# A hybrid decoder layer: eight gate tiles ahead of attention by four units of seven products, and attention's steps rearranged

## What is computed

```python
proj = u @ w_in                      # xp | q | k | v | gate_logits (2 x 1024)
y_pool = causal_pool_mixer(xp, ...) @ w_branch_pool
# strictly causal stick-breaking attention, per head and row block:
z = q @ k.T * scale
log_a = log_sigmoid(z) + cumsum_from_right(log_sigmoid(-z)) - log_sigmoid(-z)
o = where(mask, exp(log_a), 0) @ v
y_sb = o @ w_branch_attn
g_pool, g_sb = split(sigmoid(gate_logits))
h = h + (g_pool * y_pool + g_sb * y_sb) @ w_out
```

## Time and profile before

| | us |
|---|---|
| median of 3 runs (1916.88 to 1917.36) | 1917.23 |
| the profiled execution | 1917.42 |
| its span, first to last instruction | 1915.6 |
| TensorE busy | 1904.6 (99%) |
| VectorE busy | 1371.4 (72%) |
| ScalarE busy | 795.7 (42%) |
| POOL busy | 117.6 (6%) |
| attention, from the first to the last gate matmul | 240.0 |

### The profile page before, as it was taken

The page is one execution under the profiler, slowest core; times in us unless marked ns, Lnnn a source line. Parts: engine busy times, 40 slices in busy tenths (PEclk is TensorE's granted clock), DMA queues, the critical chain, the costliest instruction groups (busy, mean ns, idle before and its releaser), DMA issues.

```text
span 1915.6 us, 24977 instructions
## 1 busy us (share of the span) xinstructions
PE 1904.6 (99%) x9010; PEld 1593.2 (83%) x9010; DVE 1371.4 (72%) x1677; ACT 795.7 (42%) x1175; POOL 117.6 (6%) x157
## 2 busy tenths in 40 slices
PE   9999999999999999999999999999999999999998
PEld 9888888888888888888888888898888888888887
DVE  6978777784565786488677768889777777756555
ACT  7423232323434544234676762474323232324344
POOL 1000000000000200000233220010000000000002
PEclk9999999999999999999999999999999999999999
DMA  5456654558676733415875447643545444677665
GB/s 165 144 199 229 224 181 140 199 188 303 213 237 203 196 110 132 132 50 160 247 173 148 128 142 257 198 138 119 178 145 194 149 168 153 218 263 244 205 193 205
DMA packets 258419, 348.24 MB, mean 182 GB/s; under 512 B 29344, under 2 KB 161184, under 8 KB 255008
## 3 DMA queue, kind: packets, MB, share of 16 engines
q1 hardware_dynamic: 258336, 347.15, 56.2%
HBM read 233.83 MB, written 112.99 MB: 181 GB/s over the span
## 4 chain that ended last, share of the span: by engine, by line
PE 96%; DVE 1%; SPq 1%; DMA 1%; issue 0%; ACT 0%; POOL 0%; POOLq 0%; DVEq 0%; ACTq 0%
PE bank L1265 40%; PE bank L1321 8%; PE bank L1322 8%; PE bank L1323 8%; PE bank L1374 8%; PE bank L1515 6%; PE bank L1217 3%; PE bank L1451 2%; PE bank L1423 2%; PE bank L1481 2%; PE bank L1587 2%; PE bank L1192 1%; PE bank L1606 1%; PE bank L1605 1%; PE bank L1572 1%; PE bank L1570 1%
## 5 line engine op out<-in xcount | busy, mean ns | idle before, releaser
L2255 DVE TENSOR_TENSOR dn_lo<-dn_lo_raw,dn_hi 128x1024 fp32r<-128x1024 f32 x149 | 181.7, 1222 | 149.9 <-ACT dn_hi L1790 149.5
L1265 PE MATMUL bank<-lo_t,wa_hi 128*128 128x512 f32 x656 | 252.8, 389 | 0.0
L1265 PE MATMUL bank<-hi_t,wa_hi 128*128 128x512 f32 x656 | 252.8, 389 | 0.0
L1265 PE MATMUL bank<-hi_t,wa_lo 128*128 128x512 f32 x656 | 252.8, 389 | 0.0
L1790 ACT ACTIVATE dn_hi<-dn_lo_raw 128x1024 fp32r<-128x1024 f32 x149 | 157.9, 1061 | 219.0 <-DMA dn_lo_raw<-act_dram 219.0
L1321 PE MATMUL bank<-dn_hi 128*128 128x512 f32 x596 | 232.6, 390 | 0.0
L1323 PE MATMUL bank<-dn_lo,dn_hi 128*128 128x512 f32 x596 | 231.9, 389 | 0.0
L1322 PE MATMUL bank<-dn_hi,dn_lo 128*128 128x512 f32 x596 | 231.9, 389 | 0.0
L1265 PE MATMUL bank<-hi_b,wa_hi 128*128 128x512 f32 x492 | 190.6, 389 | 0.9 <-DVE up L2389 0.9
L1265 PE MATMUL bank<-hi_b,wa_lo 128*128 128x512 f32 x492 | 190.4, 389 | 0.0
L1265 PE MATMUL bank<-lo_b,wa_hi 128*128 128x512 f32 x492 | 190.4, 389 | 0.0
(11 more groups left out here) (275 smaller groups left out, 3750.9 us busy)
## 6 DMA issues: line engine op xcount, KB each, us to landing
wa_lo_raw<-in_ffn_w_gate_up_dram SPq DMA_DIRECT2D x87, 512.0 KB, 5.0
dn_lo_raw<-act_dram SPq DMA_DIRECT2D x149, 256.0 KB, 4.4
act_dram<-g SPq DMA_DIRECT2D x44, 512.0 KB, 4.5
wd_t<-in_ffn_w_down_dram SPq DMA_DIRECT2D x44, 512.0 KB, 6.6
act_dram<-s_of SPq DMA_DIRECT2D x88, 256.0 KB, 6.5
wd_dram<-wd_t SPq DMA_DIRECT2D x22, 1024.0 KB, 6.0
dn_lo_raw<-wd_dram SPq DMA_DIRECT2D x85, 256.0 KB, 3.3
dn_lo_raw<-in_ffn_w_down_dram SPq DMA_DIRECT2D x64, 256.0 KB, 3.0
```

The source lines that it names most:

```text
L1265: last = nc.tensor.matmul(acc, lhs, rhs, start=n == 0 and i != 2 and i < 5, stop=n == 11, skip_group_check=True)
L2255: return nc.vector.tensor_tensor(dst, raw, hi.bitcast(f32), ALU.subtract)
```

## The change

`EARLY` goes from 4 to 8: all eight tiles of the attention gate come out of mix units (four gate units instead of two), and the sixteen banks that stay in attention are all gates of the pool branch. A fourth row buffer `a3` is added and `LAG` is 3: transposes, `at_hi` and `at_lo` of a tile come three steps behind its logits instead of two, and the weighing moves with them. VectorE does `at_lo` ahead of the scan in every step. The shares of the first three steps, of the steps with value work on VectorE and of the last steps are raised. The first keys of the first head are loaded by ScalarE's queue instead of SP's, and the last pool branch tiles are stored ahead of a gate weight's load. In the first feed-forward VectorE's first Strassen pair is written out in an order of its own.

```diff
-EARLY = 4
+EARLY = 8
...
-DRAIN = 4
-V_DIFF, V_HIGH, V_LOW = ({NT + 3 + d: 1, 3 * NT + 3 + d: 2, 5 * NT + 3 + d: 3} for d in (0, 1, 5))
+DRAIN = 5
+LAG = 3
+V_DIFF, V_HIGH, V_LOW = ({NT + 4 + d: 1, 3 * NT + 4 + d: 2, 5 * NT + 4 + d: 3} for d in (0, 1, 2))
...
-HEAD_SHARE = 16
+HEAD_SHARE = 28
...
-    shares = [SHARE[x["qt"]] for x in TILES] + [7] * DRAIN
+    shares = [SHARE[x["qt"]] for x in TILES] + [12] * DRAIN
     shares[0] += HEAD_SHARE
-    shares[1] += 8
+    shares[1] += 14
+    shares[2] += 8
+    for s in (*V_DIFF, *V_LOW):
+        shares[s] += 5
...
+        a3 = at("a3", [P, SEQ], f32, G0)
...
-                    for dst, part in ((k_hi2, 0), (k_lo2, 1)):
+                    for dst, part in ((k_hi2, 0), (k_lo2, 1)) if hn or c0 else ():
...
+            spill_pool_branch(3)
             gate_unit(1)
-            spill_pool_branch(3)
             load_head(1)
...
             def weights_of(n):
-                return a2[:, :] if n % 3 == 2 else a[:, n % 3, :]
+                return (a[:, 0, :], a[:, 1, :], a2[:, :], a3[:, :])[n % 4]
...
-                if s >= 4 and s % 2 == 0:
-                    weigh((s - 4) // 2)
-                if 2 <= s < NA + 2:
-                    turn(s - 2)
+                if s >= LAG + 2 and s % 2:
+                    weigh((s - LAG - 2) // 2)
+                if LAG <= s < NA + LAG:
+                    turn(s - LAG)
...
+            def load_first_keys():
+
+                for i in range(3):
+                    act.wait_ge(ring_sp[i], 32 * ring_uses(i))
+                act.wait_ge(pool_prod, 6 * (KT // 2 - 1) + 3)
+                for dst, part in ((k_hi2, 0), (k_lo2, 1)):
+                    for half in (slice(0, 64), slice(64, P)):
+                        act.dma_start(dst[half, 0, 0:HALF].bitcast(f32),
+                                      qk_dram[part, PAIR_ORDER[0], 0:64, SEQ:SEQ + HALF]).then_inc(head_in[0], 16)
+
+            load_first_keys()
...
-                if n >= 3:
-                    act.wait_ge(t_ok, CHUNKS[n - 2])
+                if n >= 4:
+                    act.wait_ge(t_ok, CHUNKS[n - 3])
...
-                    with dve.Fori(1, WO_PAIRS + 1) as i:
+                    first_strassen_pair(even, odd, units)
+                    with dve.Fori(2, WO_PAIRS + 1) as i:
...
+            def first_strassen_pair(even, odd, units):
+
+                c11(0, 2, 0)
+                weight_sums(0, 3, odd, units + 2)
+                c22_first(0, 2, 0)
+                weights_lo(0, 3, odd)
+                c22_second(0, 2, 0)
+                sums_lo(0, 3, odd)
+                unit_end(0, 2, 1, 0, 0)
+                up_unit(0, 3, 1, 1, more=(even, units + 3), use=1)
...
-                turned_first = 2 <= s <= NA and TILES[s - 1]["qt"] in (1, 5, 3)
-                if turned_first:
-                    turned_lo(s - 2)
+                if LAG <= s < NA + LAG:
+                    turned_lo(s - LAG)
                 if 1 <= s <= NA:
                     weigh_keys(s - 1)
-                if 2 <= s < NA + 2 and not turned_first:
-                    turned_lo(s - 2)
```

More of the change, by code:

```diff
@@ L1108, in _ @@
                         store_gate(fb)
-                    if s == NA:
+                    if s == NA + 1:
                         move_o(NA // 2 - 2, 3, slice(0, HALF // 2))
-                    elif s == NA + 2:
+                    elif s == NA + 3:
                         move_o(NA // 2 - 1, 4, slice(HALF // 2, HALF))
-                    elif s >= 4 and s % 2 == 0:
-                        store_o((s - 4) // 2)
+                    elif s >= LAG + 2 and s % 2:
+                        store_o((s - LAG - 2) // 2)
                     if s == O_STEP:
@@ L1118, in _ @@
                             sp_.wait_ge(o_sp[b], 32 * (NA // 4 - 2))
[L1119 to L1122, removed]
+                    if O_STEP <= s < O_STEP + 5:
+                        load_output(s - O_STEP, slice(0, P if s < O_STEP + 3 else 64))
                     if s == NA:
@@ L2204, in _ @@
             for s in range(NA + DRAIN):
[L2205 to L2208, removed]
+                if s >= LAG + 2 and s % 2:
+                    take_o((s - LAG - 2) // 2)
+                if LAG <= s < NA + LAG:
+                    turned_hi(s - LAG)
                 if s < NA:
```

## The result

The changed kernel takes **1923.36 us** (median; 1921.34 to 1924.02) against 1917.07 (1916.74 to 1917.36) of the kernel before, measured beside it: ratio 1.0031, 95% interval 1.0022 to 1.0040, **6.3 us slower**. The forecast was 2.1 us faster, and the time lies outside its range.

What follows compares the result with a forecast made beforehand. TensorE's list of matmuls was taken as the time. Products -5.44, first pair -1.11, present waits -1.54 and new waits +6.0 gave -2.1 on 1917.42: 1915.3, median 1915.1 us; forecast's own range 1913.4 to 1919.6, 8 in 10 1910.3 to 1919.6.

Steps and rivals of the forecast that it cites:

- Products, mix units, first pair: Gate products leave attention, two gapless mix units added: net -5.4 us; reordered first Strassen pair in first feed-forward: -1.1 us.
- third rival: Added mix units wait for stores of reused ring tiles, losing 1 to 2 us each: 1918; chance 0.04.
- Start of attention, 0.5 us: ScalarE's first weight copy waits for its late transfer, with the transposes' copies queued behind it: 0.5 us.
- The clock: TensorE's granted clock should stay at its upper level, 2.4 GHz, since no wait is longer than a step.
- key wait: At attention's start, the 0.6 us wait on a key transfer goes once ScalarE issues the first four.
- Steady waits, 1.6 + 1.6 + 1.8 + 0.5: Waits through attention: weighing of fifth and sixth tile, two wide tiles in a row, value splits, VectorE scans running long.
- Place A: Weighing of a head's fifth and sixth row tile: short by 0.2 us a head, 1.6 in all.
- Place B: Two wide tiles in a row, a head's first and second: short by 0.2 us, 1.6 in all.
- the splits: Three value splits on VectorE in attention: 0.8 us short each, partly caught by slack, 1.8 us in all.
- The first, VectorE keeping up: Rival: mean load of 89% leaves room, attention's waits stay at 4.2 us or less, 1910.7; chance 0.36.
- The second: Rival: POOL's 16 products collide with VectorE's scans in attention, 16 us of waits, 1925; chance 0.08.
- the tenths recur eight times: Argument against VectorE keeping up: places A and B fall short by tenths, repeated over the eight heads.

Runs made afterwards that it cites:

- a_start: Changed kernel with the start of attention as before (keys back on SP ahead of queries, gate weights ahead of last pool stores): 1924.71 us.
- a_early4: Changed kernel with four gate tiles ahead of attention instead of eight, the rest as changed: 1913.16 us against 1917.18 of the kernel before, ratio 0.9980.
- a_late2: Changed kernel with ScalarE's four copies of gate unit 1's weights one step later: 1920.60 us.
- a_dose: The changed kernel with weight copies one step later, plus every fourth gate matmul of attention run twice (96 matmuls more): 1931.78 us.
- a_late: Changed kernel with ScalarE's four copies of gate unit 1's weights moved later, first piece at gate matmul 44 instead of 26: 1925.91 us.
- a_idle: Changed kernel with VectorE's scans cut to 128 columns per row tile and ScalarE's first sigmoid to 128 per chunk: 1916.88 us.

## Why the prediction was wrong

- **Products, mix units, first pair.** Right: 24 matmuls fewer, 152.3 us of mix stage, 1.0 to 1.1 us for the pair. The third rival (waits in mix units) didn't occur.
- **Start of attention, 0.5 us.** This term failed first. I had the right queue (a late transfer, the weight copy, the `at_hi` behind it) and gave it at most twice the 0.56 us of the earlier trace rows. The copy waited 3.42, TensorE 2.53 plus 1.7 for the clock, plus 1.5 on `q_st`: 5.7 us in the profile. The term has no length for the transfer, which took 7.2 us before; with four stores ahead of it and ScalarE's keys beside it, it took 10.7. And I had not set the thin opening against SP's timetable: whatever SP sends last arrives too late for it, as a_start shows.
- **The clock.** It was to stay at its upper level, "since no wait is longer than a step". A wait of 2.53 us, not longer than a mean step (23.4 / 8 = 2.9 us), was followed by 3.4 us at half of it, a loss that the forecast had at nothing.
- **`q_st`.** The key wait of 0.6 went, but what is late next is the query transfer, at 1.5. Moving the keys to another queue won nothing: TensorE starts its second logits 4.66 us after the start of attention here, and also 4.66 in a_start, with the keys on SP. The DMA share is 1.02 to 1.14 in that stretch (946 to 960).
- **Steady waits, 1.6 + 1.6 + 1.8 + 0.5.** 5.5 us were forecast and some 12 came. Place A, the weighing of the fifth and sixth tile, was the wrong place: it waits in two heads only (0.4 and 0.6). In a head where it does not wait (transposes at 1021.70), the `at_lo` ends 1.75 us behind the transposes (1023.94 against 1022.19), just as before and in spite of the scan ahead, with 1.94 of cover. The transposes just ahead of that weighing come 0.23 late in every head, 1.8 us, and the weighing of the last two tiles costs 0.46 in six heads and 1.1 in the first, 3.9 us; I had neither. Place B cost some 1.1 us in the seven heads behind the start's hole and the splits some 2, near what I had; the weighing of a head's first two tiles, 0.8 in all, I had not. And I counted a wait as the lateness of one matmul: a late weighing also costs 0.1 on the next, and transposes inside a set lose hundredths that no row shows as idle.
- **The whole.** Attention takes 210.2 us where I had 201, 9.2 more; the profiled execution missed its forecast by 8.7 (1924.0 against 1915.3). So the miss lies in attention. Against a_early4's (237.5 us, less 43.5 of products: 194.0) it holds 16 us of loss, where I had 6.0 of waits.
- **Rivals.** The first, VectorE keeping up, was right that the mean load leaves room and wrong about what follows from it. The load was 79%, not 85 to 90: a head took some 23.4 us, not 21.9, and VectorE's work in it about 18.6, not 19.4. The second gave 1925, near the time, for another reason: POOL is 1.3 us at most. I had no rival in which cover itself runs out for all places at once. My argument against the first rival, "the tenths recur eight times", was that mechanism, priced as a sum of two places.

What stays open: how the 12 us of steady loss divide exactly. The runs give 3.7 to 4.6 to VectorE's scans, 1.2 to ScalarE's sigmoids and 0.2 to 1.3 to POOL, leaving some 5 to 7. Of these the transposes of the sixth tile, 1.8, are shown to be the chain of hand-overs alone; for the rest that is argued. The shares need not add up, since one relief changes the others' waits.

## What to carry to other kernels

When independent work is taken out of a stage where it covers a chain between engines, price the whole stage by that chain, not by the engines' mean loads: with VectorE 82% busy between 1000 and 1050 us in a_late2, which leaves room, attention lost 13 us, and with 79% and a quarter more gate matmuls in a_dose two. Here the loss had a threshold, so try half the step before the whole one: the rearrangement here is worth 4.0 us with four early tiles and is eaten with eight. And price a wait from start to start: a wait shown as 0.20 us idle cost 0.46.

## What the runs showed of the hardware that I had not expected

A stop of TensorE of about the same length brought a fall of the granted clock in some runs and none in others. After 2.5 us in the changed kernel it was 0.50 for 3.4 us; after 2.2 us in a_start it stayed at its upper level:

```profile
960.00:962.00 2.00, 0.27 (x2) 1.00 0.94 225
962.00:964.00 2.00, 1.56 (x11) 1.00 1.04 260
```

In a_dose a stop of 2.1 us at the first logits did bring one, as did one of 3.6 in a_late, and in a_idle one of 2.4 didn't. So the length of a stop alone does not tell here whether it costs the clock. Nor does the kernel: over the whole span five of the changed kernel's eight executions were granted 0.998, like the profiled one, and took 1923.04 to 1924.02, three 0.999 and 1921.34 to 1922.83; of a_start's five the profiled one alone was granted 0.999. That the executions at 0.998 have such a fall is shown only where they were profiled.
